# Delta rule: broadcasting decay sums and beta by masked rows and 32-row products instead of by 24 products with a repeated column

## The reference, cut to what matters

```
beta = sigmoid(b_raw)
g    = -exp(a_log) * softplus(a_raw + dt_bias)
gc   = cumsum(g)                       # within a chunk, per head
decay[i, j] = exp(gc[i] - gc[j])  for i >= j, else 0
kb    = k * beta
lower = strict(kb @ k.T * decay)
intra = incl(q @ k.T * decay)
```

## Time and profile before

| | us |
|---|---|
| median of 3 executions (2449.15 to 2450.02) | 2449.47 |
| the profiled execution, its own time | 2449.32 |
| its span, first to last instruction | 2447.5 |
| PE busy | 2414.6 |
| DVE busy | 1657.7 |
| ACT busy | 1250.9 |

### The profile page before, as it was taken

The page is one execution under the profiler, slowest core; times in us unless marked ns, Lnnn a source line. Parts: engine busy times, 40 slices in busy tenths (PEclk is TensorE's granted clock), DMA queues, the critical chain, the costliest instruction groups (busy, mean ns, idle before and its releaser), DMA issues.

```text
span 2447.5 us, 34157 instructions
## 1 busy us (share of the span) xinstructions
PE 2414.6 (99%) x14580; PEld 2139.5 (87%) x14580; DVE 1657.7 (68%) x1895; ACT 1250.9 (51%) x1378; POOL 0.2 (0%) x4
## 2 busy tenths in 40 slices
PE   8999999999999999999999999999999999999997
PEld 8999988899999888988888888878888888888876
DVE  5788758557887585667657577565657667667764
ACT  5554256455543565544444344456556465565573
POOL 0000000000000000000000000000000000000000
PEclk9999999999999999999999999999999999999999
DMA  6543223555532335555555555555454555555553
GB/s 235 207 175 137 98 109 130 198 206 199 182 138 90 118 130 198 195 189 189 189 189 189 189 189 189 194 206 191 153 186 179 193 183 189 189 177 185 203 193 121
DMA packets 63977, 428.17 MB, mean 175 GB/s; under 512 B 7121, under 2 KB 7249, under 8 KB 14801
## 3 DMA queue, kind: packets, MB, share of 16 engines
q1 hardware_dynamic: 61280, 414.97, 47.6%
q10 hardware_dynamic: 2544, 11.01, 1.2%
HBM read 421.76 MB, written 4.19 MB: 174 GB/s over the span
## 4 chain that ended last, share of the span: by engine, by line
PE 97%; DVE 1%; ACT 1%; issue 0%; DMA 0%; DVEq 0%; SPq 0%; ACTq 0%
PE PS L421 95%; PE PS L547 1%; PE PS L652 1%; DVE X L1627 0%; PE PS L643 0%; PE PS L785 0%; ACT Q L977 0%; ACT WH L991 0%; PE PS L766 0%; DVE SM L1642 0%; DVE Q L1627 0%; DVE O L1623 0%; DMA W<-in_wall 0%; DVE H L1623 0%; DVE Y L1623 0%
## 5 line engine op out<-in xcount | busy, mean ns | idle before, releaser
L1658 DVE TENSOR_TENSOR WL<-W,WH 128x2048 fp32r<-128x2048 f32 (+2 forms) x392 | 860.4, 2203 | 505.7 <-ACT WH L991 505.3
L991 ACT ACTIVATE WH<-W 128x2048 fp32r<-128x2048 f32 (+2 forms) x392 | 718.0, 1842 | 506.4 <-PE PS L421 421.1
L421 PE MATMUL PS<-H,WH 128*128 128x256 f32 (+1 forms) x4864 | 946.5, 327 | 0.0
L421 PEld LDWEIGHTS PS<-H,WH 128*128 128x128 f32 x4864 | 713.0, 191 | 43.9
L421 PE MATMUL PS<-H,WL 128*128 128x256 f32 x3392 | 558.3, 284 | 7.6 <-DVE H L1627 7.6
L421 PEld LDWEIGHTS PS<-H,WL 128*128 128x128 f32 x3392 | 503.2, 190 | 50.9 <-issue 9.2
L421 PE MATMUL PS<-WH,H 128*128 128x512 f32 (+1 forms) x1280 | 331.1, 379 | 0.0
L421 PEld LDWEIGHTS PS<-WH,H 128*128 128x128 f32 x1280 | 234.1, 188 | 46.1
L421 PE MATMUL PS<-WH,YS 128*128 128x512 f32 x1024 | 273.8, 389 | 0.0
L421 PEld LDWEIGHTS PS<-WH,YS 128*128 128x128 f32 x1024 | 192.2, 188 | 40.0
L421 PE MATMUL PS<-WL,H 128*128 128x512 f32 (+1 forms) x640 | 197.2, 387 | 5.3 <-DVE H L1623 5.3
(11 more groups left out here) (146 smaller groups left out, 1598.9 us busy)
## 6 DMA issues: line engine op xcount, KB each, us to landing
W<-in_wall SPq DMA_DIRECT2D x374, 1024.0 KB, 4.8
W<-in_wall SPq DMA_DIRECT2D x24, 512.0 KB, 3.5
W<-in_wall SPq DMA_DIRECT2D x8, 536.0 KB, 3.6
X<-in_xT SPq DMA_DIRECT2D x8, 256.0 KB, 5.4
X<-in_x ACTq DMA_DIRECT2D x1, 2048.0 KB, 10.6
xsave<-X ACTq DMA_DIRECT2D x1, 2048.0 KB, 8.3
X<-xsave ACTq DMA_DIRECT2D x1, 2048.0 KB, 11.9
Q<-in_g_post ACTq DMA_DIRECT2D x8, 256.0 KB, 3.4
```

The lines of the kernel that those rows point to most:

```text
L421: return e.matmul(o, l, r, start=start, stop=stop, skip_group_check=True)
L991: e.activation(WH[:, s % NSPL, 0:m], W[:, c % NRAW, 0:m], ACT.Copy).then_inc(*up("hi", c))
L1658: e.tensor_tensor(WL[:, c % NRAW, 0:m], W[:, c % NRAW, 0:m], WH[:, s % NSPL, 0:m].bitcast(F32), ALU.subtract).then_inc(*up("lo", c))
```

## The change

g and beta are also copied to a new tile `SPR` (zeroed once): group r of 32 columns holds the four g of units 4r to 4r+3 in its columns 0 to 3 and the four beta in columns 4 to 7. One product of `SPR` with `cum` then gives the rows gc of all units at partitions 32r+c (key `gr`), and one of `SPR` with `ident` the rows of beta (key `br`). DVE multiplies such a bank by a mask table `pick` (new in `TB`), four times side by side, into an SBUF tile of 128x512 (`RG` or `RB`) that has in each 32-row group only one row that is not zero for each block of 128 columns. Then one product with 32 rows of ones and 512 columns for each of the three row groups broadcasts four units at once: three products in place of twelve.

PE now waits twice where it did not: for `("dn_v", l, "gr")` before `eg` and for `("dn_v", l, "br")` before `bt`. The product `gr` stands at pump 11 together with `gc`, which moves there from pump 13 with its wait for g; `br` stands at pump 39. On DVE `rows_of` stands at pump 11 and at pump 39.

```diff
+    c["pick"] = (i[:, None] < 96) & (i[:, None] % 32 == i[None, 0:8])
...
+        SPR = SM[:, 320:448]
+        spread = SPR.rearrange("p (r c) -> p r c", r=4)
...
+        RG, RB = KD[:, 0:512], KD[:, 512:1024]
...
             def decays(l):                      # PE
-                yield from rest(12)
+                yield from rest(10)
                 w.wait_ge(*to("dn_v", l, "g"))
+                b = side(("dn", l, "gr"), ("dn_v", l, "gr"))
+                mm(b[:, 0:128], SPR, tbl("cum")).then_inc(*up("dn_p", l, "gr"))
                 b = side(("dn", l, "gc"), ("dn_v", l, "gc"))
                 mm(b[:, 0:12], tbl("cum"), gs[:, 12:24])
                 mm(b[:, 16:28], ones, gs[:, 12:24], start=False).then_inc(*up("dn_p", l, "gc"))
+                yield from rest(2)
+                w.wait_ge(*to("dn_v", l, "gr"))
                 for k in range(3):
                     b = side(("dn", l, "eg", k), ("dn_v", l, "di", k), ("dn_a", l, "eg", k))
-                    for j in range(4):
-                        u = 4 * k + j
-                        i = mm(b[:, 128 * j:128 * j + 128], gs[:, 12 + u:13 + u].to_broadcast([128, 128]),
-                               tbl("cum"), start=(j == 0))
-                    i.then_inc(*up("dn_p", l, "eg", k))
+                    ks = slice(32 * k, 32 * k + 32)
+                    mm(b, ones[ks, :], RG[ks, :]).then_inc(*up("dn_p", l, "eg", k))
...
             def delta_net(l):                   # PE
-                yield from rest(11)
+                yield from rest(9)
+                b = side(("dn", l, "br"), ("dn_v", l, "br"))
+                mm(b[:, 0:128], SPR, ident).then_inc(*up("dn_p", l, "br"))
+                yield from rest(2)
+                w.wait_ge(*to("dn_v", l, "br"))
                 for k in range(3):
                     b = side(("dn", l, "bt", k), ("dn_v", l, "kb", k))
-                    for j in range(4):
-                        u = 4 * k + j
-                        i = mm(b[:, 128 * j:128 * j + 128], gs[:, u:u + 1].to_broadcast([128, 128]), ident,
-                               start=(j == 0))
-                    i.then_inc(*up("dn_p", l, "bt", k))
+                    ks = slice(32 * k, 32 * k + 32)
+                    mm(b, ones[ks, :], RB[ks, :]).then_inc(*up("dn_p", l, "bt", k))
...
+            def rows_of(dst, key, c, *sig):     # DVE
+                pick = TB[:, AT["pick"] + c:AT["pick"] + c + 4]
+                tt(quad(dst), sbank(*key)[:, 0:128].unsqueeze(1).to_broadcast([128, 4, 128]),
+                   pick.unsqueeze(2).to_broadcast([128, 4, 128]), ALU.mult, *sig)
...
             def decays(l):                      # DVE
+                copy(spread[:, 0:3, 4:8], bt.rearrange("p (r c) -> p r c", r=3))
...
+                copy(spread[:, 0:3, 0:4], gs[:, 12:24].rearrange("p (r c) -> p r c", r=3), "dn_v", l, "g")
-                yield from rest(10)
+                yield from rest(8)
+                w.wait_ge(*to("dn_p", l, "gr"))
+                rows_of(RG, ("dn", l, "gr"), 0, "dn_v", l, "gr")
                 w.wait_ge(*to("dn_p", l, "gc"))
                 copy(pair(gs[:, 36:60]), ...)
                 tt(kdw, gls, gcs, ALU.subtract, "dn_v", l, "kdw")
+                yield from rest(2)
...
             def delta_net(l):                   # DVE
-                yield from rest(5)
+                yield from rest(3)
+                w.wait_ge(*to("dn_p", l, "br"))
+                rows_of(RB, ("dn", l, "br"), 4, "dn_v", l, "br")
+                yield from rest(2)
```

More of the change, by code:

```diff
@@ L1827, in decays @@
                 g3 = gs[:, 12:24].rearrange("p (h t) -> p h t", h=6)
-                tt(g3, g3, gs[:, 24:30].unsqueeze(2).to_broadcast([128, 6, 2]), ALU.mult, "dn_v", l, "g")
-                yield from rest(10)
+                tt(g3, g3, gs[:, 24:30].unsqueeze(2).to_broadcast([128, 6, 2]), ALU.mult)
+                copy(spread[:, 0:3, 0:4], gs[:, 12:24].rearrange("p (r c) -> p r c", r=3), "dn_v", l, "g")
+                yield from rest(8)
+                w.wait_ge(*to("dn_p", l, "gr"))
+                rows_of(RG, ("dn", l, "gr"), 0, "dn_v", l, "gr")
                 w.wait_ge(*to("dn_p", l, "gc"))
@@ L2040, in block1 @@
                 if not l:
+                    zero(SPR)
                     rope_tables()
```

## The result

The changed kernel takes 2472.63 us (median of 4, 2470.29 to 2473.16) against 2449.56 for the kernel before: a ratio of 1.0093, 95% interval 1.0077 to 1.0109. That is 23 us slower. The profiled execution has a span of 2470.4 us.

A forecast was written before the change was run, and what follows sets the result against it. PE, busy 99% of the span and 97% of the last-ending chain, was taken to bound the kernel. 2449.3 + 15.2 (waits less shorter trios, four places) + 5.6 (clock) = 2470 us, range 2461 to 2478.

The forecast's parts named there:

- The mechanism: At both places, DVE is behind PE in the program, so PE must wait for DVE's masking (`rows_of`).
- The lengths of the waits: PE stands about 3.1 to 3.3 us at place 1 (g, pump 13), 6.5 at place 2 (beta, pump 41).
- The trio: Three new products at each place run side by side: 1.08 us after a wait, replacing 2.67 to 2.76 us.
- The row of 64 rows: Trace row of four heads' scores, alternating between two strips: 1.61 us against 2.6 one after the other; basis for overlap.
- The wait for g: Place 1, pump 11: two copies delay g's signal, so PE waits 0.5 us, contained in the longer wait.
- The clock: Granted clock falls to half in each place 2 wait, not at place 1: twice 2.8, +5.6 us.
- the gap of before: PE's 5.43 us stand until 1733.76 in the old trace; clock fell 4.2 us into it, 2.8 us lost.
- Case 1: Rival: the waits come, the clock stays or loses little at each place; 2464.5 us, chance 0.20.
- Case 2: Rival: strips do not run side by side, or only in program order; 2473 to 2477 us, chance 0.12.
- Case 3: Rival: DVE finishes masking before PE arrives, so PE only has the shorter list; 2444.5 us, chance 0.06.
- PE waits for nobody between place 2 and the layer's last steps: After place 2 in each layer: nothing later gives back the lost time, so the four places make +15.2 us.

The follow-up runs named there:

- e6: Changed kernel with its new work and both waits, but the twelve old products at each of the four places instead of three new ones: 2478.87 us.
- e8: Changed kernel with three numbers changed, so PE's trios come three pumps later at place 1 and five at place 2; DVE's list unchanged: 2448.99 us.
- e3: Changed kernel with products nobody reads put before the waits, three at place 1 and seven at place 2: 2463.63 us.
- e7: e1 with one more edit, the transposes of the keys one pump later on PE: 2443.59 us.
- e10: e7 with all products of a trio on rows 0 to 31, one strip, so part of the computation is changed: 2450.60 us.
- e2: Changed kernel with all products of a trio on rows 0 to 31, one strip, so part of the computation is changed: 2489.00 us.
- e1: Changed kernel with the rows of beta made at place 1 and the trio of g three pumps later (pump 16): 2446.83 us.

## Why the prediction was right, point by point

**The mechanism.** Forecast: PE waits for DVE's masking, since DVE's list reaches pump 39 and pump 11 later than PE comes to pumps 41 and 13. Shown by the waits (four times, for L1629), by e6 (waits without the new products lose more), and by e8 (PE asks later, the loss is gone).

**The lengths of the waits.** Forecast 3.1 to 3.3 and 6.5 us; measured 2.97, 6.53, 2.97, 6.51. The delays less the trios' gain were put at 2.30, 5.33, 2.21 and 5.33, together 15.2; e3, where the clock plays no part, shows 2.35, 5.38, 1.99 and 5.38 (15.1). The pairing of pumps and the chain from the last `QA` to the masking were thus right to 0.2 us at each place. The latency from the masking's end to PE's first record was 0.05, not 0.15, but the masking itself started 0.1 later after its predecessor than assumed, and the two cancel.

**The trio.** Forecast 1.08 us after a wait at full clock; e3 shows 222.18 - 0.24 - 220.78 = 1.16. Forecast 0.1 to 0.2 more without a wait; e7 shows 1.17 and 0.09 of entry (the trio is due at 210.58 + 0.48 = 211.06 and starts at 211.15), 1.26. The row of 64 rows was the right neighbour. The Trainium skill (TensorE: Matmul & The Clock Gate, "Part 3: Packing small matmuls") has matmuls start and end strictly in program order. If the two records of one product stand together in that order, the six records would be four deep and the trio would take 1.72 us and the edges. The trace disagrees for records in different strips: 1.17 us.

**The wait for g.** Forecast 0.5 us at place 1; measured 0.24 in layer 0 and none in layer 1 (it was contained in the longer wait, so nothing hung on it).

**The clock: the term that was mis-sized.** Forecast 5.6 us: a fall in each wait at place 2, none at place 1. Measured as the difference between the changed kernel and e3: 9.0 us (8.7 from the table's steps: 1.6 and 2.5 in layer 0, 2.8 and 1.8 in layer 1). So place 2 cost 4.3 us and not 5.6, and place 1, which had been put at nothing, 4.4. The clock fell at place 1 too, within 0.4 us of PE's resuming, though the wait of 3.0 us is well short of the 4.2 us after which it had fallen in the gap of before. The step that failed is to take the time of one fall in one gap as a bound: at place 2 of layer 0 it fell by 218.0, 2 us into the wait. The size for each fall, 2.8 us, was a good upper value (1.6 to 2.8 were measured). The sum of 2470 lies as near to 2472.6 as it does partly by luck: the clock's two errors have opposite signs, and 1.2 us came back near 1738.

**The rivals.** Case 1 (clock stays) is what e3 made, 2463.6 for a forecast of 2464.5, but the kernel as changed is not that. Case 2 (no overlap) is refuted by e10. Its price was also too low, since it took the slow trios at full clock: e2, which is that case, took 2489, and not the 2473 to 2477 stated for it. Case 3 (DVE in time): e7 is that case, and 2443.6 was measured for a forecast of 2444.5. The working's 2.7 - 1.08 - 0.2 - 0.22 = 1.2 for each place was right: in the table e7 gains 0.97, 1.42, 1.01 and 1.42 at the places, 4.8 together. But the working said nothing of the transposes, where without a further edit over half of the gain (e1) to nearly all of it (e8) is given back; and 0.7 us of e7's 5.7 come at the gap near 1738, where a different part of the half clock fell on work. "PE waits for nobody between place 2 and the layer's last steps" was true of the kernel before, and hid that it was in time at the transposes by less than 0.3 us.

## What to carry to other kernels

When a chain of work of two engines is paired by counting steps, the count says nothing of time: before a wait is added, read in the timeline when the other engine stands at that step, and put the consumer behind it. A wait on the engine that bounds the kernel cost twice here, where it was 3 us or longer: once by its length and once by the clock that fell with it. Filling it took back the clock's part (9 of 23 us), and moving the asking point by three numbers in the source took back both. And a gain on the bounding engine is only kept if the next place at which it meets another engine has room: look for the meeting points without idle time, not only for those with.

## What the runs showed of the hardware

- Three fp32 products of 32 rows and 512 columns in three row strips took 1.17 us with the exit, and 0.09 of entry, against 2.86 us on the same measure in one strip (e7, e10). Each fp32 product is two records, and the strips' records ran side by side.
- The granted clock fell to 0.5 after waits of PE of only 3.0 us (place 1 of both layers), and cost 1.6 and 2.8 us there. At the same wait lengths the time at half speed differed from layer to layer: 3.4 and 6.8 us after place 1, 10.2 and 6.8 at place 2. With products in the wait (0.5 us of rest left) it never fell at the places, and it did not fall in the waits of 1.1 and 1.5 us at the transposes (e1, e8).
- The half clock also stretches what stands right behind the wait: 24 records took 5.4 us instead of 2.8 (e6), and a trio 2.0 instead of 1.1.
